# Hybrid attention and convolution encoder layer: two seven-product feed-forward pairs instead of one, attention and convolution in denser slots

## The reference

```python
h = rms(x, norm1_g)
q, k, v, c = split(h @ w_in)               # 512, 128, 128, 1024 columns
q, k = rms(q), rms(k)                      # per head of 64; 8 query heads, 2 key heads
attn = window_attention(q, k, v, sink)     # |distance| <= 128, ALiBi, blocks of 128 queries
u = a * sigmoid(gate)                      # a, gate = halves of c
u = silu(layernorm(dwconv31(u)))
x += concat(attn, u) @ w_out
h2 = rms(x, norm2_g)
x += (silu(dwconv3(h2 @ w_gate)) * (h2 @ w_up)) @ w_down    # 2816 hidden channels
```

## Time and profile before

| | |
|---|---|
| median of three runs | 2665.61 us (2664.36 to 2668.46) |
| the profiled execution: first to last instruction | 2660.9 us |
| slots (input, output projections, plain windows) | to 2105.1 us |
| pair, first to last product | 2105.1 to 2649.6 us |
| granted TensorE clock, mean | 0.998 |
| data moved | 453.73 MB, mean 171 GB/s |
| matmuls | 13,191 |

### The profile page before, as it was taken

How to read it: one execution, slowest core, us unless ns; L and a number is a source line. 1 busy time by engine, 2 the same in 40 slices (tenths; PEclk the granted TensorE clock), 3 DMA queues, 4 the chain that set the end, 5 groups by cost and what they waited for, 6 DMA issues and landing times.

```text
span 2660.9 us, 35240 instructions
## 1 busy us (share of the span) xinstructions
PE 2631.4 (99%) x13191; PEld 2337.7 (88%) x13191; DVE 1820.6 (68%) x3020; ACT 1258.5 (47%) x2031; POOL 192.8 (7%) x332
## 2 busy tenths in 40 slices
PE   8999999999999999999999999999999999999998
PEld 6777777788889988889998889998899999999998
DVE  4775658787686876676876677876257576765764
ACT  6345464566454447345446345446144333533432
POOL 0110021100110000010000010000000000000001
PEclk9999999999999999999999999999999999999999
DMA  9967679633843444843443853433745521222211
GB/s 332 349 227 249 249 280 361 231 128 125 298 165 117 156 132 135 290 167 115 157 136 123 291 169 120 157 129 132 284 157 174 177 64 60 68 65 63 68 52 66
DMA packets 138761, 453.73 MB, mean 171 GB/s; under 512 B 24449, under 2 KB 37121, under 8 KB 121953
## 3 DMA queue, kind: packets, MB, share of 16 engines
q1 hardware_dynamic: 111616, 349.17, 39.0%
q0 software_dynamic: 26976, 102.32, 10.5%
HBM read 362.63 MB, written 88.79 MB: 170 GB/s over the span
## 4 chain that ended last, share of the span: by engine, by line
PE 93%; DVE 3%; issue 1%; DMA 1%; ACT 1%; SPq 0%; POOL 0%; DVEq 0%; ACTq 0%; POOLq 0%
PE bank L2131 31%; PE bank L2147 16%; PE bank L2277 12%; PE bank L2083 12%; PE bank L2117 8%; PE bank L2293 7%; PE bank L2231 2%; PE bank L2209 2%; PE bank L2220 2%; DMA wraw<-w_in_t 1%; DVE weights L1561 0%; PE bank L2176 0%; DMA weight_scratch<-weights 0%; ACT weights L1147 0%; ACT part_hi L1404 0%
## 5 line engine op out<-in xcount | busy, mean ns | idle before, releaser
L2131 PE MATMUL bank<-hw_hi,weights 128*128 128x440 f32 (+1 forms) x2816 | 812.2, 365 | 0.0
L2131 PEld LDWEIGHTS bank<-hw_hi,weights 128*128 128x128 f32 x2816 | 530.0, 188 | 47.9 <-issue 12.9
L2131 PE MATMUL bank<-hw_lo,weights 128*128 128x440 f32 (+1 forms) x1408 | 510.8, 363 | 0.0
L2147 PE MATMUL bank<-mid,weights 128*128 128x438 f32 x2112 | 431.9, 364 | 0.0
L1561 DVE TENSOR_TENSOR weights<-wraw,weights 128x1024 fp32r<-128x1024 f32 x286 | 348.8, 1220 | 117.0 <-ACT weights L1147 116.8
L2147 PEld LDWEIGHTS bank<-mid,weights 128*128 128x128 f32 x2112 | 396.0, 189 | 33.3 <-issue 7.6
L1147 ACT ACTIVATE weights<-wraw 128x1024 fp32r<-128x1024 f32 x286 | 301.5, 1054 | 256.9 <-DMA wraw<-w_down_t 171.2
L1668 DVE SCALAR_TENSOR_TENSOR cc<-win,par,cc 128x512 f32<-128x512 f32 x600 | 414.5, 744 | 0.0
L2083 PE MATMUL bank<-h_hi,weights 128*128 128x512 f32 x1104 | 358.6, 398 | 2.9 <-DVE weights L1561 2.9
L2131 PEld LDWEIGHTS bank<-hw_lo,weights 128*128 128x128 f32 x1408 | 264.4, 188 | 16.6 <-issue 1.0
L2083 PEld LDWEIGHTS bank<-h_hi,weights 128*128 128x128 f32 x1104 | 207.9, 188 | 56.0 <-issue 8.3
(11 more groups left out here) (213 smaller groups left out, 3688.0 us busy)
## 6 DMA issues: line engine op xcount, KB each, us to landing
weights<-weight_scratch SPq DMA_DIRECT2D x88, 1024.0 KB, 5.9
wraw<-w_ffn_t SPq DMA_DIRECT2D x176, 512.0 KB, 3.5
wraw<-w_down_t SPq DMA_DIRECT2D x88, 512.0 KB, 3.5
weight_scratch<-weights POOLq DMA_DIRECT2D x22, 1024.0 KB, 8.3
part_raw<-w_ffn_t SPq DMA_DIRECT2D x88, 256.0 KB, 2.6
part_raw<-w_pass_t SPq DMA_DIRECT2D x44, 256.0 KB, 2.6
cat_hi<-cat_scratch SPq DMA_DIRECT2D x10, 1024.0 KB, 6.6
cat_lo<-cat_scratch SPq DMA_DIRECT2D x10, 1024.0 KB, 9.0
```

What stands on the lines that cost most here:

```text
L2131: mm = nc.tensor.matmul(out, l[:, k, :], r[:, k, 1:TC + 1] if s else r[:, k, :], start=(k == 0 and j == 0), stop=(k == KT - 1 and j == 2))
L2147: mm = nc.tensor.matmul(out, l[:, q, :], mid[:, k, part, :], start=(k == 0 and j == 0), stop=(k == FH - 1 and j == 2))
```

## The change

Two of the four plain windows go, and a second pair comes: `PLAIN, PAIRS` = 2, 2. Columns of a plain window become 450 (452 read), of a pair's window 416 (418 read). There are 242 slots instead of 374, and the order is written out anew: `O` of chunks 1 to 3 stands between halves, `O` of chunk 4 between the last `G` and the last `D` phase. Attention, convolution and layer norm of chunks 1 to 4 get new places: blocks are 9 slots apart instead of 10 or 20, transposes come three a slot, the values after slot b+9, and the layer norm of every chunk is in the short form. Between the pairs the window sums and splits are placed by `WINDOW_STEPS`. The high parts get a ring of four. Keys and values are loaded by two calls with a semaphore each. Chunk 4's x2 has a buffer of its own, and many buffers are placed anew; the waits that this needs are added.

```diff
-PLAIN, PAIRS = 4, 1
-TP = 406
+PLAIN, PAIRS = 2, 2
+TP = 416
...
-for _w in range(PLAIN):
-    PHASES.append(("F", _w, 0))
-    if _w + 1 < CHUNKS:
-        PHASES.append(("O", _w + 1))
-    PHASES.append(("F", _w, 1))
+PHASES += [("G", 0, 0), ("D", 0, 0), ("O", 1), ("G", 0, 1), ("D", 0, 1), ("O", 2)]
+PHASES += [("G", 1, 0), ("D", 1, 0), ("O", 3), ("G", 1, 1), ("O", 4), ("D", 1, 1)]
...
-ATTN_AT = {0: (16, 10), 1: (59, 10), 2: (103, 20), 3: (178, 20), 4: (252, 20)}
-CONV_AT = {0: (12, 47), 1: (58, 96), 2: (108, 165), 3: (181, 240), 4: (256, 312)}
+ATTN_AT = {0: (16, 10), 1: (57, 9), 2: (101, 9), 3: (139, 9), 4: (180, 9)}
+CONV_AT = {0: (12, 47), 1: (58, 84), 2: (95, 133), 3: (144, 172), 4: (182, 209)}
 LN_SUM = {c: 1 if c == 1 else 0 for c in CONV_AT}
-LN_STEPS = {c: tuple(LN_SUM[c] + i for i in ((1, 1, 2, 2, 3, 3, 4, 4, 5) if c < 2 else (1, 2, 3, 4, 5, 6, 7, 8, 9)))
+LN_STEPS = {c: tuple(LN_SUM[c] + i for i in (1, 1, 2, 2, 3, 3, 4, 4, 5))
             for c in CONV_AT}
...
-        POOL_SIDE[_b - 2].append(("load_kv", _c))
+        if _c > 0:
+            POOL_SIDE[_b - 2].append(("load_k", _c))
+        POOL_SIDE[_b + 1].append(("load_v", _c))
...
-        PE_SIDE[_b + 7 + _i // 2].append(("transpose", _N, _g, _k))
-        ACT_SIDE[_b + 8 + _i // 2].append(("copy_t", _N, _g, _k))
-    PE_SIDE[_b + 10].append(("values", _N))
-    ACT_SIDE[_b + 11].append(("attn_high", _N))
-    DVE_SIDE[_b + 11].append(("attn_low", _N))
-    POOL_SIDE[_b + 11].append(("attn_store", _c, _n))
+        PE_SIDE[_b + 7 + _i // 3].append(("transpose", _N, _g, _k))
+        ACT_SIDE[_b + 8 + _i // 3].append(("copy_t", _N, _g, _k))
+    PE_SIDE[_b + 9].append(("values", _N))
+    ACT_SIDE[_b + 10].append(("attn_high", _N))
+    DVE_SIDE[_b + 10].append(("attn_low", _N))
+    POOL_SIDE[_b + 10].append(("attn_store", _c, _n))
...
+WINDOW_STEPS = [(-7, "sum T1"), (-6, "low B11"), (-6, "sum T2"), (-5, "low T1"), (-5, "sum T3"), (-4, "sum T4"),
+                (-3, "low T2"), (-3, "low B21"), (-2, "low B22"), (-1, "low T3"), (0, "low T4")]
...
-HI_RING, DOWN_RING = 5, 4
+HI_RING, DOWN_RING = 4, 4
...
-        for _i, _t in enumerate(("T1", "T2", "T3", "T4")):
-            DVE_AT[_n - 6 + _i].append(("window_sum", _q, _t))
         for _i, _b in enumerate(B_ORDER):
-            ACT_AT[_n - 6 + _i].append(("window_high", _q, _b))
-            DVE_AT[_n - 6 + _i].append(("window_low", _q, _b))
+            ACT_AT[_n - 7 + _i].append(("window_high", _q, _b))
+        for _i, _w in WINDOW_STEPS:
+            DVE_AT[_n + _i].append(("window_sum" if _w[:3] == "sum" else "window_low", _q, _w[4:]))
...
-LAST = START["F", PLAIN - 1, 1]
-PAIR_LOADS = {LAST + 10 + i: b for i, b in enumerate(("B11", "B12", "B22", "B21"))}
+LAST = START["G", PLAIN - 1, 1]
+LAST_O = START["O", CHUNKS - 1]
+PAIR_LOADS = {LAST_O + 2: ["B12"], LAST_O + 3: ["B22"], LAST_O + KT - 1: ["B11", "B21"]}
...
+PAIR_DVE = {LAST_O + KT + i: t for i, t in (
+    (1, [("sum", 0, "S1"), ("sum", 0, "S2"), ("sum", 0, "S3"), ("sum", 0, "S4")]),
+    (2, [("window_sum", 0, "T1")]), (3, [("window_sum", 0, "T2"), ("window_low", 0, "B11")]),
+    (4, [("window_sum", 0, "T3")]), (5, [("window_sum", 0, "T4")]),
+    (6, [("window_low", 0, "T1")]), (7, [("window_low", 0, "T2")]), (9, [("window_low", 0, "B21")]))}
...
-        x2, = run(R_X, ("x2", [P, KT, TB], F32))
+        x2_first, = run(R_X, ("x2", [P, KT, TB], F32))
+        x2_last, = run(R_SIDE - H, ("x2_last", [P, KT, TB], F32))
+        x2 = [x2_first] * (CHUNKS - 1) + [x2_last]
...
+            def load_k(c):
+                pool.wait_ge(s_qk, GROUP * BLOCKS * c)
...
+            def load_v(c):
                 if c > 0:
-                    pool.wait_ge(s_qk, GROUP * BLOCKS * c)
                     pool.wait_ge(s_pv, BLOCKS * c)
...
                 if k >= HI_RING:
                     act.wait_ge(s_used, SLOTS + k - HI_RING + 1)
+                else:
+                    act.wait_ge(s_mlo, H_PLAIN)
...
+                if n == 0:
+                    pe.wait_ge(s_vl, 16 * (c + 1))
```

More of the change, by code:

```diff
@@ L95 @@
         SLOT += [("O", _p[1], o) for o in range(KT)]
+    elif _p[0] == "G":
+        SLOT += [("G", _p[1], _p[2], i // 2, i % 2) for i in range(GU_TILES)]
     else:
-        SLOT += [("G", _p[1], _p[2], i // 2, i % 2) for i in range(GU_TILES)]
         SLOT += [("D", _p[1], _p[2], i) for i in range(D_TILES)]
@@ L611, in encoder_layer @@
-        m_at = R_MID
-        y_at = [R_MID + M_BYTES + Y_BYTES * i for i in range(2)]
-        b_at.append(R_HW - B_BYTES)
-        assert R_D + 4 * B_BYTES + 3 * E_BYTES <= R_MID and R_HW + 13 * W_BYTES <= R_SIDE
-        assert v_at[2] + V_BYTES <= R_D and R_SM <= b_at[13] and y_at[1] + Y_BYTES <= b_at[13]
-        b_raw, b_lo, b_hi = {}, {}, {}
-        for i, b in enumerate(B_ORDER):
-            lo_at, hi_at = b_at[i], b_at[7 + i]
-            b_raw[b], = run(lo_at, (f"{b}_raw", [P, KH, TQ], F32))
-            b_lo[b], = run(lo_at, (f"{b}_lo", [P, KH, TQ], F32R))
-            b_hi[b], = run(hi_at, (f"{b}_hi", [P, KH, TQ], F32R))
@@ L622, in encoder_layer @@
-        b_raw["B12"] = b_raw["T3"]
-        w_place = {("A", 0, a): i for i, a in enumerate(("A11", "S1", "S2", "A12", "S4", "S3"))}
-        w_place["A22", 0] = 6
-        w_hi_at = w_at[7:7 + HI_RING]
-        w_rest = w_at[7 + HI_RING:]
-        w_places = [("A", 1, a) for a in ("A11", "S1", "S2", "A12", "S4", "S3")] + [("A22", 1), ("A22", 2)] + \
-            [("D", i) for i in range(DOWN_RING)]
-        w_offset = {k: w_at[i] for k, i in w_place.items()}
-        w_offset.update({k: w_rest[i] for i, k in enumerate(w_places)})
+        LATE = R_SIDE - H
@@ new lines, in encoder_layer @@
+        ring_end = B_BYTES + 11 * W_BYTES
+        late_end, side_end = LATE + 3 * B_BYTES, R_ATTN + 6 * B_BYTES
+        lo_at = dict(zip(B_ORDER, [R_D + B_BYTES * i for i in range(4)] + [R_ATTN + B_BYTES * i for i in range(3)]))
+        hi_at = dict(B11=R_ATTN + 3 * B_BYTES, T1=R_ATTN + 4 * B_BYTES, T2=R_ATTN + 5 * B_BYTES, B21=LATE, B22=0,
+                     T3=LATE + B_BYTES, T4=LATE + 2 * B_BYTES)
+        e_at = [R_D + 4 * B_BYTES + E_BYTES * i for i in range(3)]
+        m_at = e_at[2] + E_BYTES
@@ new lines, in encoder_layer @@
+        y_at = [m_at + M_BYTES + Y_BYTES * i for i in range(2)]
+        w_hi_at = [R_SM + W_BYTES * i for i in range(HI_RING)]
+        w_first = [R_SM + W_BYTES * (HI_RING + i) for i in range(5)] + [side_end, side_end + W_BYTES]
+        w_rest = [B_BYTES + W_BYTES * i for i in range(11)] + [late_end]
+        v_at = [ring_end, late_end + W_BYTES, side_end + 2 * W_BYTES, y_at[1] + Y_BYTES]
+        assert ring_end + V_BYTES <= R_D and w_first[4] + W_BYTES <= LATE and R_SM + HI_RING * W_BYTES >= R_HW
@@ new lines, in encoder_layer @@
+        assert v_at[1] + V_BYTES <= R_ATTN and v_at[3] + V_BYTES <= R_SM
+        b_raw, b_lo, b_hi = {}, {}, {}
+        for b in B_ORDER:
+            b_raw[b], = run(lo_at[b], (f"{b}_raw", [P, KH, TQ], F32))
+            b_lo[b], = run(lo_at[b], (f"{b}_lo", [P, KH, TQ], F32R))
+            b_hi[b], = run(hi_at[b], (f"{b}_hi", [P, KH, TQ], F32R))
+        b_raw["B12"] = b_raw["T3"]
+        w_offset = dict(zip([("A", 0, a) for a in ("A11", "S1", "A12", "S3")] + [("A22", 0), ("A", 0, "S2"), ("A", 0, "S4")], w_first))
@@ L632, in encoder_layer @@
+        w_offset.update(zip([("A", 1, a) for a in ("A11", "S1", "S2", "A12", "S4", "S3")] + [("A22", 1), ("A22", 2)] +
+                            [("D", i) for i in range(DOWN_RING)], w_rest))
         p_raw, p_lo = {}, {}
@@ L909, in load_down @@
                     sp.wait_ge(s_used, SLOTS)
+                    sp.wait_ge(s_h2st, x2_stores(CHUNKS - 1))
                 else:
@@ L992, in _ @@
                         load_residual(c)
-                if n in PAIR_LOADS:
-                    load_pair_window(0, PAIR_LOADS[n])
+                for b in PAIR_LOADS.get(n, ()):
+                    load_pair_window(0, b)
                 if n == LAST + GU_TILES:
@@ L1347, in x2_square @@
                     act.wait_ge(s_n2a, (KT - 1) * c)
-                nc.scalar.activation(sq[o % 2][:], x2[:, o, :], ACT.Square).then_inc(s_x2q, 1)
+                nc.scalar.activation(sq[o % 2][:], x2[c][:, o, :], ACT.Square).then_inc(s_x2q, 1)
             def norm2_scale(c):
@@ L1830, in part_sum @@
                     dve.wait_ge(s_used, SLOTS)
+                elif gi == 0 and a == "S1":
+                    dve.wait_ge(s_ast, 32 * BLOCKS * CHUNKS)
                 two = {"S1": ("A21", "A22"), "S2": ("S1", "A11"), "S3": ("A21", "A11"), "S4": ("A12", "S2")}[a]
```

100 lines of the change are left out of this document (49 added, 51 removed), and 3 rows, old and new, of the table PAIR_DVE.

## The result

The changed kernel takes **2700.9 us** (median of four runs, 2700.7 to 2701.2), the kernel before 2665.0 beside it: 1.3% slower, ratio 1.013 with an interval of 1.0117 to 1.0142. The forecast was 2646 and faster; the range ended at 2668. The profiled execution has a span of 2699.1 us.

What follows compares the result with a forecast made beforehand. The prediction took TensorE's streaming as the bound: -49.7 us there, plus 33 us of waits coming back, 30 net of the 2.9 that leave, gives -19.7 us, so 2665.6 becomes 2646 us. The range was 2622 to 2668.

Steps and rivals of the forecast that it cites:

- What TensorE gives up: Two plain windows gone (-634.5 us), wider columns (+15.8 and +12.2), a second pair (+556.8): net -49.7 us.
- The ring of four: Ring of weight parts in the pairs, four instead of five: ScalarE still writes parts in time, no cost.
- (a): Output projection of chunk 3, slots 196 to 200: VectorE's surplus over TensorE costs 8 us (0 to 10.6).
- (b): Output projection of chunk 2, slots 156 to 159: VectorE's surplus over TensorE costs 5 us (0 to 7.1).
- (c): Slots 144 to 148, down products with convolution steps and window low parts: VectorE's surplus costs 3 us (0 to 5.4).
- (d): Chunk 1's layer norm beside attention block 7, slots 85 to 93: VectorE and ScalarE late, 7 us (1 to 10).
- (e): Chunk 4's layer norm beside attention block 19, slots 210 to 216, with narrow bands: 3 us (0 to 6).
- (f): Layer norms of chunks 2 to 4: squares, their adds and variance matmul share one slot, 3 us (0 to 6).
- (g): Three transposes and copies a slot, values one slot earlier: hidden by ScalarE's slack, else up to 6 us; 2 taken.
- Rival 2: From slot 60 on VectorE becomes the bound at 89% busy and the kernel ends slower, 2673 us; chance 0.09.
- Rivals 1: The denser slots hide the surpluses: 8 to 14 us of stalls, 2621 to 2627 us; chance 0.22.
- main case: The forecast holds, 2632 to 2660 us, TensorE's waits from 130 us to the first pair 12 to 55; chance 0.56.

Runs made afterwards that it cites:

- run 12: Changed kernel, blocks 10 slots apart, two transposes a slot, output additions, bias and ScalarE's copies first, convolution laid out anew, layer norm sums later: 2639.2 us.
- run 2: Changed kernel with the output additions of the pairs' first down pass ahead of the weight parts on VectorE's queue: 2687.2 us.
- run 1: Kernel before with a ring of four high parts of weights in the pair instead of five, nothing else changed: 2672.2 us.
- Run 5: Changed kernel with chunk 1's second norm and chunk 2's variance one slot later, so no two results share the PSUM bank in a slot: 2691.8 us.
- run 7: Changed kernel with attention blocks at an even step of 10 slots, two transposes a slot, values one slot later, late norm sum in chunk 3: 2684.3 us.
- run 4: Kernel before with four long stops put into TensorE's queue, each a chain of three small transfers: 2706.4 us.
- run 14: Kernel before with four short stops put into TensorE's queue, one small transfer each: 2686.3 us.
- run 8: Changed kernel with the edits of run 2 and run 7 and the convolution levelled by measured lengths, chunk 1's late sum as in the changed kernel: 2682.5 us.
- run 10: The kernel of run 7 with the output additions first, as in run 2, and the scores' bias first on VectorE's queue: 2671.5 us.

## Why the prediction was wrong

**What TensorE gives up** was right: -49.7 us. Both paces were met within 1 ns, and in run 12 some 27 of the 49.7 us show as time. The Trainium skill (TensorE: Matmul & The Clock Gate, Back-to-back issue gap) gives N/2.4 + 2.5 ns for an isolated matmul, by estimate 190.0 ns at 450 columns; the row has 205.5, so the trace disagrees here as it did before.

**The ring of four** is the step that failed outright. The prediction said that it "still lets ACT write product k+3 as soon as product k-1 is done, three products of 2.2 us ahead" and costed it at nothing. It asked whether the parts come in time for their own product; they do. It did not ask what stands behind them on VectorE's queue. In the first down pass the part of product k+4 is ahead of the additions of product k, for whose banks TensorE's next product waits. Measured: 12.2 us of waits in both pairs, 13.7 with what follows (run 2), 7.6 for one pair (run 1). That is most of the 19 us of the pair stage.

**VectorE's surpluses (a) to (c)** were right in place and about in size. Excess over the bare pace, clock included: 10.0 us at slots 197 to 199 (8 forecast), 6.4 at 157 to 159 (5), 3.0 at slot 149 (3). At slot 198 the way was another than the prediction had it, over ScalarE to the values. Two sites of the kind were missed: 6.5 us at 76 to 78, where the first window's low parts stand, and 5.8 at 173, where the first sum of chunk 3's layer norm waits 3.9 us for VectorE behind convolution steps. A third missed site is the load at slot 62: 2.1 us of wait, about 4 with the lower clock behind it.

**(d) and (e)**, ScalarE beside a layer norm: 6.6 us at slots 92 and 93 (7 forecast), 3.3 at 210 and 214 (3).

**(f) and (g)** were mis-sized. "Hidden by 1 to 2 us of ACT slack, else up to 6; I take 2" was the wrong end and too low an end: the three transposes in a slot, the values a slot earlier and the shared bank took 2.6 us at slot 23, 3.9 at 53 and 54, 7.0 at 118 and 119, and (f) 3.1 at 137, some 17 us where 5 were taken. The first two sites lie in slots 0 to 55, which the prediction had called unchanged. The prediction had costed the copies and had listed neither what stands ahead of them on ScalarE's queue nor who else uses the values' bank. Run 5 gives 9.1 us for the bank alone and run 7 16.6 for the layout (chunk 3's later sum in it), even with more VectorE surplus.

**The granted clock** had no term. The slot stage lost at most 17 us by it, which are in the sizes above, and the first waits of the pairs a few more. So the sum of the waits is not the price of the waits: by runs 4 and 14 a stop of 4 us costs 5, one of 8 costs 10.

Together: the slot stage gave back 66.8 us (the excess over the bare pace, 79.5 from slot 10 on, less 12.7 in the kernel before) where 28 net were forecast, the pair stage 19. That is 58 us for the 54.9 between 2700.9 and 2646; the 3 us left are start, end and rounding. **Rival 2** named the right sign and came nearest with 2673, but not its mechanism: VectorE did not become a bound at 89% busy, for in run 12 it does the same work and the slot stage is 44 us shorter (TensorE's first pair product starts 1508.9 us into the span, where it was 1553.1). It was lateness at certain items. Rivals 1, 3, 4 and 5 fell: the first products of the second pair did not wait 10 us, table loads show no drain, and columns cost no step. The signs that the prediction gave did not tell: TensorE's waits between 130 us and the first pair are 49.1 us, inside the main case's 12 to 55. They watched neither the clock nor the first down passes, and their upper limit stood 22 us above the 33 that the sum had.

What run 12 does not settle is how the 62 us between it and the changed kernel split by cause; runs 8 and 10 show that they don't add up, since a wait taken away at one site lets VectorE or ScalarE be late at the next. Some 22 us of the 49.7 have not come back even in run 12. Whether the kernel before would gain from the same order was not tried; it has 2.9 us of such waits.

## What to carry to other kernels

When a change makes slots denser, list for each slot the items that another engine waits for in the same slot, and sum what is ahead of them on their queue, uncounted items too; a planner that levelled the load without knowing these brought nothing here. When a ring is shortened, ask not only whether its own user is in time but what else is queued behind the instruction that now waits. Put items wanted at once ahead of those wanted two slots later, and add to each remaining stop of TensorE what its clock costs.

## What the hardware showed that was not expected

TensorE's granted clock fell from the upper to the lower level at single stops in an otherwise full queue: 0.50 over three microseconds behind a stop of 3.8 us in run 14, 0.52 over seven at the longer gaps of the changed kernel. Each short stop of run 14 cost about 1.1 us beyond its length and each of 8.4 us in run 4 about 2.0. The length of the stop alone does not decide. The changed kernel has drops at waits of 2.0 to 5.1 us, and run 1 has none at three waits of 2.0. At slot 149 TensorE waited 2.9 us both in the changed kernel and in run 2; behind it only the second, whose queue is the same there, shows the drop (first row the changed kernel, second row run 2):

```profile
992.00:996.00 4.00, 4.00 (x21) 3.67 (x21) 3.90 (x12) 1.76 (x6) 0.56 (x1) 1.00 0.41 160
992.00:996.00 4.00, 4.00 (x14) 3.51 (x13) 3.90 (x12) 1.91 (x7) 0.55 (x1) 0.59 0.56 224
```

No run here shows what decides it. The kernel before, with waits of at most 1.1 us in its slot stage, has no drop between 60 and 2600 us; the changed one has eleven.
